# Score products with K's low part: two 64-row tiles in place of two 128-row products

## The reference

```python
q = rms_norm(q.reshape(B, S, H, 2, d), q_norm_w)      # d = 64
k = rms_norm(k.reshape(B, S, H, 2, d), k_norm_w)
...
s = jnp.einsum('bhcqd,bhckd->bhcqk', qblk, kt).astype(f32) * scale
p = jax.nn.softmax(s, axis=-1)
a = p[:, :, 0] - lam * p[:, :, 1]
return jnp.einsum('bhqk,bhke->bhqe', a.astype(vh.dtype), vh)
```

## Time and profile before, and how to read it

| | |
|---|---|
| median of three runs | 826.01 us |
| profiled execution: span | 824.4 us |
| PE matmul busy | 802.7 us (97%), 3616 matmuls |
| PE weight loads (PEld) busy | 662.8 us (80%), 3616 loads |
| DVE busy | 468.4 us (57%) |
| ACT busy | 364.6 us (44%) |
| DMA moved | 89.12 MB |

### The profile page before, as it was taken

The page is one execution under the profiler, slowest core; times in us unless marked ns, Lnnn a source line. Parts: engine busy times, 40 slices in busy tenths (PEclk is TensorE's granted clock), DMA queues, the critical chain, the costliest instruction groups (busy, mean ns, idle before and its releaser), DMA issues.

```text
span 824.4 us, 10257 instructions
## 1 busy us (share of the span) xinstructions
PE 802.7 (97%) x3616; PEld 662.8 (80%) x3616; DVE 468.4 (57%) x694; ACT 364.6 (44%) x590; POOL 2.5 (0%) x5
## 2 busy tenths in 40 slices
PE   3799999999999999999999999999999999999998
PEld 3688888888888888888888888888888888888886
DVE  5628775772686667428775672686668643232322
ACT  6544445542454634454346543454644542222220
POOL 1000000000000000000000000000000000000000
PEclk9899999999999999999999999999999999999999
DMA  9233622213244222233622223254212464424331
GB/s 339 82 103 102 179 77 78 69 59 127 76 127 129 74 76 76 77 101 102 178 76 76 76 70 108 81 144 130 66 63 77 128 204 153 146 88 148 102 102 51
DMA packets 69525, 89.12 MB, mean 108 GB/s; under 512 B 4481, under 2 KB 53889, under 8 KB 68993
## 3 DMA queue, kind: packets, MB, share of 16 engines
q1 hardware_dynamic: 67632, 86.72, 33.8%
q10 hardware_dynamic: 1874, 2.18, 0.9%
HBM read 78.39 MB, written 4.19 MB: 100 GB/s over the span
## 4 chain that ended last, share of the span: by engine, by line
PE 96%; DVE 2%; ACT 1%; DMA 1%; issue 0%; DVEq 0%; ACTq 0%
PE ps L292 94%; PE ps L382 2%; DVE mixed L663 1%; DVE h_lo L653 1%; DMA mixed<-in_x 1%; ACT at_hi L468 0%; PE ps L354 0%; DVE mixed L856 0%; PE ps L284 0%; ACT h_hi L461 0%; ACT x_rms L471 0%; DVE x_rstd L662 0%; DVEq L852 0%; DVEq L661 0%; ACTq L466 0%
## 5 line engine op out<-in xcount | busy, mean ns | idle before, releaser
L669 DVE TENSOR_TENSOR w_lo<-raw,w_hi 128x512 fp32r<-128x512 f32 x256 | 175.5, 690 | 300.4 <-ACT w_hi L483 297.8
L483 ACT CAST w_hi<-raw 128x512 fp32r<-128x512 f32 x256 | 158.7, 622 | 374.0 <-PE ps L292 373.0
L292 PE MATMUL ps<-h_hi,w_hi 128*128 128x512 f32 x768 | 303.0, 395 | 1.8 <-DVE h_lo L653 1.8
L292 PE MATMUL ps<-h_lo,w_hi 128*128 128x512 f32 x768 | 300.4, 391 | 0.0
L292 PE MATMUL ps<-h_hi,w_lo 128*128 128x512 f32 x768 | 205.9, 390 | 0.0
L292 PEld LDWEIGHTS ps<-h_hi,w_hi 128*128 128x128 f32 x768 | 144.8, 189 | 31.8 <-ACT w_hi L483 2.2
L292 PEld LDWEIGHTS ps<-h_hi,w_lo 128*128 128x128 f32 x768 | 144.4, 188 | 30.6
L292 PEld LDWEIGHTS ps<-h_lo,w_hi 128*128 128x128 f32 x768 | 144.9, 189 | 29.6
L292 PE MATMUL ps<-w_hi,h_hi 128*128 128x512 f32 x256 | 99.7, 389 | 0.0
L292 PE MATMUL ps<-w_hi,h_lo 128*128 128x512 f32 x256 | 99.6, 389 | 0.0
L292 PE MATMUL ps<-w_lo,h_hi 128*128 128x512 f32 x256 | 99.6, 389 | 0.0
(11 more groups left out here) (105 smaller groups left out, 584.3 us busy)
## 6 DMA issues: line engine op xcount, KB each, us to landing
raw<-in_w_in SPq DMA_DIRECT2D x96, 512.0 KB, 3.6
raw<-in_w_out SPq DMA_DIRECT2D x32, 512.0 KB, 3.8
mixed<-in_x SPq DMA_DIRECT2D x8, 1024.0 KB, 6.9
out<-mixed SPq DMA_DIRECT2D x3, 1024.0 KB, 6.5
kh_twice<-kh_twice SPq DMA_DIRECT2D x8, 256.0 KB, 5.3
kl_twice<-kl_twice SPq DMA_DIRECT2D x8, 256.0 KB, 6.0
q_stack<-v_hi SPq DMA_DIRECT2D x8, 256.0 KB, 3.6
wp_raw<-in_w_pool ACTq DMA_DIRECT2D x4, 256.0 KB, 3.3
```

The lines of the kernel that those rows point to most:

```text
L292: last = nc.tensor.matmul(dst, lhs, rhs, start=first and i == 0, stop=final and i == len(pairs) - 1, skip_group_check=True)
L483: nc.scalar.copy(w_hi[:, h % W_SLOTS, :], raw[:, unit % RAW_SLOTS, part * 512:part * 512 + 512]).then_inc(w_hi_ready, 1)
L669: nc.vector.tensor_tensor(w_lo[:, h % W_SLOTS, :], raw[:, unit % RAW_SLOTS, part * 512:part * 512 + 512], w_hi[:, h % W_SLOTS, :].bitcast( ...
```

## The change

The low product of each component takes only the 64 rows that hold Q's high part and K's own low part. So for K's low part only Q's high part is multiplied; the product of the two low parts falls away. The two high products come first, then the two low products, one over rows 0 to 63 and one over rows 64 to 127, each into its component's PSUM bank. The two copies of K's low part between the halves are gone, so `k_moved` counts to 32 a round and no longer 64, and PE waits for `k_low_ready` before item 0's scores.

```diff
@@ -202,9 +202,6 @@
                     sp.wait_ge(qk_hi_ready, rnd * 4 + 2)
                     sp.dma_start(kh_twice[64:128, 0].bitcast(F32), kh_twice[0:64, 0].bitcast(F32)).then_inc(k_moved, 16)
                     sp.dma_start(kh_twice[0:64, 1].bitcast(F32), kh_twice[64:128, 1].bitcast(F32)).then_inc(k_moved, 16)
-                    sp.wait_ge(k_low_ready, rnd * 2 + 2)
-                    sp.dma_start(kl_twice[64:128, 0].bitcast(F32), kl_twice[0:64, 0].bitcast(F32)).then_inc(k_moved, 16)
-                    sp.dma_start(kl_twice[0:64, 1].bitcast(F32), kl_twice[64:128, 1].bitcast(F32)).then_inc(k_moved, 16)
 
@@ -360,15 +357,20 @@
                         if i == 0:
                             pe.wait_ge(q_moved, r * 32 + 32)
-                            pe.wait_ge(k_moved, r * 64 + 64)
+                            pe.wait_ge(k_moved, r * 32 + 32)
+                            pe.wait_ge(k_low_ready, r * 2 + 2)
                             pe.wait_ge(rstd_ready, r * 4 + 2 + START)
                         else:
                             pe.wait_ge(exp_done, r * (2 * ITEMS) + 2 * i)
                         for c in range(2):
 
-                            stacked = q_stack[:, c, h, t * P:(t + 1) * P]
-                            last = products(ps[:, S0 + c, :], [(stacked, kh_twice[:, c, h, :]),
-                                                               (stacked, kl_twice[:, c, h, :])], True, True)
+                            products(ps[:, S0 + c, :], [(q_stack[:, c, h, t * P:(t + 1) * P], kh_twice[:, c, h, :])],
+                                     True, False)
+                        for c in range(2):
+
+                            own = slice(64 * c, 64 * c + 64)
+                            last = products(ps[:, S0 + c, :], [(q_stack[own, c, h, t * P:(t + 1) * P],
+                                                                kl_twice[own, c, h, :])], False, True)
                         last.then_inc(scored, 1)
```

## The result

The changed kernel took 830.22 us, the median of five runs (830.02 to 831.85), against 826.01 us before, a ratio of 1.0058 with a 95% interval of 1.0047 to 1.0069. The forecast was 822.7 us. Like for like the change costs 5.6 us, or 0.7%. The profiled execution after, at the upper level, spans 830.0 us and took 831.85 us, 5.6 us more span than before.

What follows compares the result with a forecast made beforehand. PE's matmul stream was taken to bound the kernel from 28 us on. 28 items x 0.12 us saved 3.3 us: span 824.4 to 821.1 us, plus some 1.6 us around it, 822.7 us median; range 819.4 to 831 us.

Steps and rivals of the forecast that it cites:

- What bounds the kernel: From 28 us on PE sets the time; changes to its stream reach the end one for one, except where it awaits ACT.
- the value chosen for the pair: Two low score products an item: streams overlap, second tile starts 0.11 us late; 0.34 us against 0.46, gaining 0.12.
- The bounds: Low pair's cost: 0.23 us side by side with weights loaded ahead, 0.88 us with the array emptying and loads exposed.
- The way back costs nothing there: From low pair to next full matmul: its 0.11 us load fits under the second tile's 0.23 us stream, costing 0.
- the second tile's load: In the low pair: weights load only once the first tile has started, so the second starts 0.11 us later.
- The third rival: Array empties at each change between 128 and 64 rows, around the low pair: slower, 828.7 to 838.5 us; chance 0.29.
- the dear version: Emptying around the low pair with loads exposed as well: pair 0.88 us, 0.43 more an item, 838.5 us.
- The first rival: Low pair at full overlap, both half loads ahead during the matmul before: 0.23 us, 819.6 us; chance 0.23.
- The second: Low products run one after the other, or tile changes cancel the overlap: within 0.2% of 826.0 us; chance 0.14.
- The edits at 0: Dropping SP's copies of K's low part and adding PE's wait for `k_low_ready`: each changes the time by 0.
- 28 of 32 items: Score savings count except in each round's item 4, where item 5's wait for ACT takes them: 28 x 0.12 = 3.3 us.
- cheap version: Emptying around the low pair, tail alone: pair 0.55 us, 0.10 more, swallowed at four item 4s by item 5's wait; 828.7 us.

Runs made afterwards that it cites:

- e5: Kernel before with the products by K's low part left out altogether, copies kept: 813.33 us, ratio 0.9846.
- e4: Changed kernel with component 1's low product left out, so one 64-row matmul an item in place of two: 830.72 us, ratio 1.0052.
- e7: Changed kernel with the pair of low products done twice in each item: 838.88 us, ratio 1.0155 against the kernel before.
- e1: Changed kernel with the copies of K's low part kept: 831.5 us, ratio 1.0063 against the kernel before.
- e3: Changed kernel with each component's low product right behind its high one, four changes of form an item, no tiles together: 851.5 us, ratio 1.0312.

## Why the prediction was wrong

**What bounds the kernel** was right: PE sets the time from 28 us on, and what its stream gained or lost went to the end. e5 moved the scores by 0.46 us an item and the end by 28 times that.

**The step that failed is the value chosen for the pair**, "a value near the lower end, 0.34 us". The bounds were 0.23 and 0.88; measured are 1.09 - 0.46 = 0.63 us, with 0.46 for the two high products. I argued from the one thing that the rows did show, that a load starts with the matmul before it, and took it for granted across the change of form too, although no row before holds such a change. "The way back costs nothing there" failed with it: the way back costs as much as the way in, 0.20 us. What I put on the second tile's load was wrong in the other direction: both tiles load together, and the second one is nearly free (e4).

**The third rival is what happened**, with 0.29 on it, and its ends, 828.7 and 838.5, hold the 831.7 of the upper level. Term by term: the tail that I took from the recorded duration, 0.39 - 0.23 = 0.16 us, was too long, since from the end of the stream to the next load there are 0.09 us; the load behind the change, 0.11, is exposed each time, as in the dear version; the two loads one behind the other, another 0.11, don't exist. So 0.09 + 0.11 + 0.23 + 0.09 + 0.11 = 0.63 us in place of 0.88. The row on the 0.11 was good: an exposed load costs what it costs behind the transposes. The point from which the rival decides, 0.23 us for the two changes together, was right as well: they cost 0.40.

**The rule of the Trainium skill** (TensorEngine Tiling (Array Packing), section Key Properties), that a change of the tiling mode drains TensorE, agrees with this case's trace, with an idle load path of 0.35 us ahead of every pair: by the rule the sum goes to the third rival. The page gives no price; here it is 0.09 us of pause and a load of 0.11 us that doesn't go ahead (whether PE really empties in the pause, or the load alone has to wait for the running product, the trace can't tell; the price is the same). The Trainium skill's other page (TensorE: Matmul & The Clock Gate, Part 3), on tiles that run side by side, is borne out by e4 and e7. I had the two against each other, but they hold together: tiles overlap with tiles, and the price is paid at the border. That transposes and products follow each other without a pause, which I counted against the rule, said nothing on it, as both are 128*128.

**The first rival** was right that the pair overlaps in full, and wrong that it costs nothing else. **The second** fell: the pair does run side by side, and the two changes cost more than that gives back.

**The edits at 0** were right. e1 with the copies and the changed kernel without them have the same span, and item 0's first high product in round 0 starts at 99.88 us, where it stood at 99.9.

**28 of 32 items** was right for a saving (e5) and for a loss (the wait fell from 1.7 to 0.8 us). The third rival's text said the same of its cheap version.

**The range** of 819.4 to 831.0 ended where half of the slower cases began. The median of 830.22 us lies in it by luck: three of the five runs were at the lower level, and at the upper one, where the runs before were, it is 831.7. What let the range reach that far was the allowance for the third rival; the chosen mechanism pointed the other way.

## What to carry to other kernels

A pair of 64-row tiles between 128-row matmuls of 512 columns saves one stream, 0.23 us, and pays 0.20 us at each of the two borders, so on its own it loses. It takes at least two pairs together between the borders for a gain (2 x 0.23 against 0.40, so an estimated 0.06 us), and here a second item's low products would need two more PSUM banks, where the kernel has all eight in use; that was not tried. Ask of a change of form what is loaded ahead across it before counting the streams that it saves.

## What the runs showed of the hardware

- A change between 128-row and 64-row matmuls costs 0.20 us either way, 0.09 of pause and 0.11 for a load that isn't hidden; four changes an item without overlap made 26 us more than before (e3, upper levels).
- Within the 64-row form loads go ahead as usual, and the loads of two tiles run together: two in 0.18 us (the changed kernel), as long as one alone (e4), and four in 0.30 us (e7).
- The first matmul behind such a border is recorded at 0.50 us, of 64 rows or of 128, and one whose weights were loaded ahead at 0.39. The difference is the 0.11 us of the load: the record includes the wait for the weights.
- The two levels go with the clock at the start of the projection. Of the stretch from 28 to 32 us the columns are: length, PE busy, PEld busy, DVE, ACT, POOL, granted clock, DMA share, GB/s. First the kernel before (upper level), then e3 (lower level):

```profile
28.00:32.00 4.00, 3.88 (x9) 3.08 (x10) 3.90 (x8) 1.67 (x2) 0.00 (x0) 0.52 0.08 15
```

```profile
28.00:32.00 4.00, 3.92 (x17) 3.26 (x18) 3.87 (x8) 2.17 (x3) 0.00 (x0) 1.00 0.07 18
```

In the one the clock stands almost throughout at 1.2 GHz, in the other at 2.4 GHz, after the same sparse transposes; the first eight matmuls start 0.43 us apart in the one and 0.23 in the other, 8 x 0.2 = 1.6 us, which is the distance of the levels. The two kernels do the same up to item 0's scores; the profiles of the other kernels at the upper level show 0.53 (e1) and 0.62 (the changed kernel) in this stretch. What differs is where the low stretch falls. In 25 to 28 us, while PE has gaps between its transposes, the granted clock was 0.51 before and 0.62 in e3, so in e3 it was over when the projection began; in the changed kernel it was 1.00 there, and fell after the projection's first matmuls (0.50 from 29 to 32 us). So a difference of under 2 us between two medians here can be the level alone, and only like levels should be compared. Only one lower-level execution has a profile, that of e3; that the same holds for the kernel before is inferred from it.
